# Other homes for squares, normalised rows, token rows and gathered rows, and a nineteenth weight buffer, in a two-layer mixture-of-experts diffusion step

## The reference

```
for l in range(2):
    mod = silu(c) @ w_ada[l] + b_ada[l]                  # 6 x 1024 values, for context and for latent tokens
    h = rms_norm(x) * (1 + scale) + shift
    o = [neighbourhood attention (8 heads), latent attention (8 heads)](h) @ w_out[l]
    x = x + gate1 * o
    h = rms_norm(x) * (1 + scale2) + shift2
    pick 2 of 16 experts for each token                   # router, best group of 4, top 2 in it
    x = x + gate2 * sum over the 2 experts of w * (silu(h @ w_gate[l, e]) * (h @ w_up[l, e])) @ w_down[l, e]
y = rms_norm(x)
```

## Time and profile before

| | |
|---|---|
| time, median of 3 runs | 1088.46 us (1087.3 to 1090.33) |
| the profiled execution: its time, its span | 1087.94 us, 1086.1 us |
| PE busy | 979.1 us (90% of the span) |
| DVE, ACT, POOL busy | 336.8, 247.5, 123.2 us |
| weight queue q1 | 289.06 MB; all queues 314.24 MB, 289 GB/s over the span |

### The profile page before, as it was taken

One profiled execution on the slowest core, in us unless ns is written; L12 is line 12 of the kernel. 1 busy time (PEld: TensorE's weight loads), 2 busy tenths in 40 slices (PEclk: granted clock), 3 DMA queues, 4 the chain that ended last, 5 costly groups with the idle time before them and its releaser, 6 DMA issues. The chain is left out here.

```text
span 1086.1 us, 14414 instructions
## 1 busy us (share of the span) xinstructions
PE 979.1 (90%) x5609; PEld 470.8 (43%) x5609; DVE 336.8 (31%) x858; ACT 247.5 (23%) x591; POOL 123.2 (11%) x140
## 2 busy tenths in 40 slices
PE   4899889998999999888589998999988999988895
PEld 2445546554443433333244554566543333333332
DVE  2200376512732112121240015753146212211225
ACT  2110155412211111111230203553031111111123
POOL 4120200000111111010013002000011111111103
PEclk8999999999999999899889999999989999999999
DMA  9952376663599999999987026667539999999992
GB/s 352 391 194 78 112 281 220 225 272 134 197 369 392 389 390 393 403 402 410 370 331 258 19 94 239 237 228 269 196 117 315 386 385 394 388 410 406 409 402 116
DMA packets 68860, 314.24 MB, mean 289 GB/s; under 512 B 7514, under 2 KB 9782, under 8 KB 47280
## 3 DMA queue, kind: packets, MB, share of 16 engines
q1 hardware_dynamic: 60304, 289.06, 69.4%
q0 software_dynamic: 7616, 21.01, 5.6%
q10 hardware_dynamic: 864, 3.15, 0.7%
HBM read 301.06 MB, written 17.53 MB: 293 GB/s over the span
## 5 line engine op out<-in xcount | busy, mean ns | idle before, releaser
L1032 PE MATMUL psum<-arena 128*64 128x512 f32 x512 | 239.1, 615 | 28.6 <-DMA arena<-in_w_up 24.7
L1035 PE MATMUL psum<-arena 128*64 128x512 f32 x512 | 239.7, 616 | 0.0
L1032 PEld LDWEIGHTS psum<-arena 128*64 128x64 f32 x512 | 69.3, 141 | 178.0 <-issue 173.6
L1088 PE MATMUL psum<-arena 128*64 128x512 f32 x512 | 118.7, 600 | 2.7 <-ACT arena L1538 1.6
L1936 DVE SCALAR_TENSOR_TENSOR arena<-arena,psum 64x512 f32<-64x512 f32 (+1 forms) x32 | 23.9, 748 | 275.5 <-ACT arena L1532 275.5
L1399 PE MATMUL psum<-arena 128*128 128x384 f32 x256 | 86.3, 491 | 0.0
L1253 PE MATMUL psum<-arena 128*128 128x384 f32 x256 | 83.5, 487 | 1.2 <-PE psum L1253 0.6
L1532 ACT ACTIVATE arena<-psum 64x512 f32<-64x512 f32 (+1 forms) x32 | 20.6, 644 | 276.1 <-PE psum L1035 276.1
L1035 PEld LDWEIGHTS psum<-arena 128*64 128x64 f32 x512 | 69.3, 141 | 0.0
L1253 PEld LDWEIGHTS psum<-arena 128*128 128x128 f32 x256 | 48.3, 190 | 36.8 <-issue 4.0
L1399 PEld LDWEIGHTS psum<-arena 128*128 128x128 f32 x256 | 47.5, 190 | 32.4 <-issue 0.7
(11 more groups left out here) (289 smaller groups left out, 1186.4 us busy)
## 6 DMA issues: line engine op xcount, KB each, us to landing
arena<-in_w_gate SPq DMA_DIRECT2D x64, 1024.0 KB, 24.2
arena<-in_w_up SPq DMA_DIRECT2D x54, 1024.0 KB, 23.0
arena<-in_w_ada SPq DMA_DIRECT2D x24, 2048.0 KB
arena<-in_w_down SPq DMA_DIRECT2D x44, 1024.0 KB, 23.0
arena<-in_w_down SPq DMA_DIRECT2D x40, 512.0 KB, 20.6
arena<-in_w_in SPq DMA_DIRECT2D x6, 2048.0 KB
arena<-in_w_up SPq DMA_DIRECT2D x20, 512.0 KB
arena<-in_w_out SPq DMA_DIRECT2D x4, 2048.0 KB
```

The source lines that it names most:

```text
L1032: ins = nc.tensor.matmul(bank[b][0:MAIN, :], hg[:, k, 0:MAIN], row(wg[half], k), start=(k == 0), stop=(k == KD - 1))
L1035: ins = nc.tensor.matmul(bank[b][MAIN:P, :], hg[:, k, 0:MAIN], row(wu[half], k), start=(k == 0), stop=(k == KD - 1))
L1088: ins = nc.tensor.matmul(bank[6][MAIN * j:MAIN * j + MAIN, :], hidT[:, c, 0:MAIN], down_row(w[half], c)[:, 512 * j:512 * j + 512], start=( ...
```

## The change

Memory is dealt out anew so that more places are free when attention ends, and one more place exists. The squares of the second norm of a layer go to `late_squares` (the keys' part of `latent_flat`), and its normalised rows straight into `hT`, where they are modulated in place. So `wide` is free when attention ends: it becomes place 13 and half of 14. Token rows `htok` move to the two result buffers and to `xg[0]`, which now lies in `hT`; so the front of `latent_flat` becomes free at the same time (places 16, 17), with some small rows as 17's other half. Place 18 is new: the rest of `hT`, the tail of `latent_flat` and `ada_rows`. Pieces for down of unit 2 are loaded before those of unit 3. The rows that come back at the end of a layer go to `extra` (places 8 to 11), the final gate and gain rows to `wide`.

```diff
-END_PLACES = (6, 7, 10, 11)
+END_PLACES = (8, 9, 10, 11)
+GATE_PLACES = (13, 14)
...
-NSMALL = 18
-SPLIT = (14, 15, 17)
-ROUND = (0, 1, 2, 3, 8, 9, 10, 11, 12, 15, 4, 5, 6, 7, 13, 14, 16, 17)
+NSMALL = 19
+SPLIT = (14, 15, 17, 18)
+ROUND = (0, 1, 2, 3, 8, 9, 10, 11, 13, 14, 12, 15, 16, 17, 4, 5, 6, 7, 18)
...
     order = gate_up(0) + gate_up(1) + down(0) + gate_up(2) + down(1)
-    for u in range(3, AHEAD):
+    order += down(2) + gate_up(3)
+    for u in range(4, AHEAD):
         order += gate_up(u) + down(u - 1)
...
-        htok = tiles(latent_flat[:, 0:3072], NT)
+        late_squares = tiles(latent_flat[:, 3072:6144], KD)
...
-        xg = [wide[:, 1024 * i:1024 * i + 1024] for i in range(2)]
+        xg = [hT_flat[:, 1024 * i:1024 * i + 1024] for i in range(2)]
+        htok = [y_sb[0], y_sb[1], xg[0]]
...
-        gate_row = [ring[:, 4 * SMALL + D * s:4 * SMALL + D * s + D] for s in range(2)]
-        gain_row = ring[:, 5 * SMALL:5 * SMALL + D]
-        end_hi = tiles(ring[:, 6 * SMALL:6 * SMALL + NT * D], NT)
+        gate_row = [wide[:, D * s:D * s + D] for s in range(2)]
+        gain_row = wide[:, 2 * D:3 * D]
+        end_hi = tiles(extra[:, 0:NT * D], NT)
...
-        y_hi = htok
-        y_lo = tiles(wide, NT)
+        y_hi, y_lo = end_hi, end_lo
...
-                flat = {12: bias_flat, 13: hT_flat, 16: latent_flat}[p][:, 0:SMALL]
+                flat = {12: bias_flat, 13: wide, 16: latent_flat}[p][:, 0:SMALL]
...
-            halves = {14: (bias_flat[:, SMALL:SMALL + 1024], hT_flat[:, SMALL:SMALL + 1024]),
+            halves = {14: (bias_flat[:, SMALL:SMALL + 1024], wide[:, SMALL:SMALL + 1024]),
                       15: (latent_in, caches_flat),
-                      17: (latent_flat[:, SMALL:SMALL + 1024], wide[:, SMALL:SMALL + 1024])}[p]
+                      17: (latent_flat[:, SMALL:SMALL + 1024], small_rows),
+                      18: (hT_flat[:, SMALL:SMALL + 1024], latent_and_rows[:, 8704:9728])}[p]
...
         def squares(n):
-            return xn if n % 2 else hT
+            return late_squares if n % 2 else hT
+
+        def normed(n):
+            return hT if n % 2 else xn
...
                 gate_up_weights(l, 2, 2)
+                down_weights(l, 1, 1)
+                down_weights(l, 2, 2)
                 sp.wait_ge(htok_ps, 2 * NT * (l + 1))
-                down_weights(l, 1, 1)
                 sp.wait_ge(ordered, l + 1)
...
-                sp.wait_ge(h_stored, 16 * NT * (l + 1))
-                sp.wait_ge(first_ps, 2 * (l + 1))
-                before = FIXED - 1
-                for u in range(FIXED, AHEAD):
+                before = ranked(FIXED)
+                gate_up_weights(l, FIXED, before)
+                for u in range(FIXED + 1, AHEAD):
...
-                sp.wait_ge(slot_free, max(loads.last(l, p) for p in (16, 17)) + 1)
+                sp.wait_ge(slot_free, max(loads.last(l, p) for p in END_PLACES) + 1)
                 for t in range(NT):
                     sp.dma_start(y_hi[:, t, :], y_rows.ap()[P * t:P * t + P, :]).then_inc(y_hi_in[t], 16)
-                    if t == 0:
-                        sp.wait_ge(xt_ps, UNITS_E * l + E_ALL)
...
+                act.wait_ge(h_stored, 16 * NT * (l + 1))          # ACT, copy_slots of unit 0
...
+                dve.wait_ge(h_stored, 16 * NT * (l + 1))          # DVE, route, before last_two
```

More of the change, by code:

```diff
@@ L664, in end_again @@
                 sp.wait_ge(stored_y, 32 * NT)
-            sp.wait_ge(slot_free, max(loads.last(DEPTH - 1, p) for p in (4, 5)) + 1)
+            sp.wait_ge(slot_free, max(loads.last(DEPTH - 1, p) for p in GATE_PLACES) + 1)
             sp.dma_start(gain_row, a["final_norm_g"].partition_broadcast(P)).then_inc(gain_in, 16)
@@ L1650, in _ @@
                         t = j // 2
[L1651 removed]
+                        act.dma_start(h_rows.ap()[P * t:P * t + P, :], htok[t]).then_inc(h_stored, 16)
                 experts(l, list(range(AHEAD)), ends=l == DEPTH - 1)
@@ L1968, in gate_diagonals @@
             def gate_diagonals():
-                dve.wait_ge(slot_free, max(loads.last(DEPTH - 1, p) for p in (4, 5)) + 1)
+                dve.wait_ge(slot_free, max(loads.last(DEPTH - 1, p) for p in GATE_PLACES) + 1)
                 each = [P, KD, P]
```

33 lines of the change are left out of this document (17 added, 16 removed).

## The result

The changed kernel takes 1081.76 us (median of 5 runs, 1079.78 to 1083.6), the kernel before, on the same chip, 1090.05 (5 runs, 1087.3 to 1091.91). The ratio is 0.9929, with a 95% interval from 0.9911 to 0.9948: faster by 7.7 us, 5.7 to 9.7. Five runs of the kernel before have their median 1.6 higher, so the gain, 7.7 for 9.3, is the fairer comparison. The profiled execution of the changed kernel took 1082.6 us with a span of 1080.8, against 1087.94 and 1086.1 before. Lines have moved: the gate product is L1038 (before L1032), the down product L1094 (L1088), SP's weight loads L560 (L552), the step behind the branch L510 (L502).

A forecast was written before the change was run, and what follows sets the result against it. Streamed weights were taken to bound the expert stage. Gains of 4.5 + 4.1 - 0.6 + 1.3 = 9.3 us from the profiled 1087.94 gave 1078.6, or 1079.2 as median (0.5 above); range 1075.0 to 1084.5.

The forecast's parts named there:

- The stream bounds the expert stage: Expert stages: streamed weights are the bound; each MB moved into idle time before ends the stage 1/0.396 = 2.5 us sooner.
- Layer 1, 4.1 us, less 0.3 for halves: Layer 1's expert stage: 1.63 MB more moved about point 0 saves 4.1 us; halved pieces cost 0.3.
- Layer 0, 4.5 us, less 0.3: Layer 0's expert stage: 1.76 MB more moved about point 0 saves 4.5 us; halved pieces cost 0.3.
- the points themselves stay where they are in time: Expert stage: points where SP sends further pieces, point 0 the first, do not shift, since PE isn't waiting for weights there.
- Halved pieces, 0.3 us a layer: Weight stream: 20 pieces a layer in halves instead of 15 make smaller packets, costing 0.3 us, from nothing to 0.5.
- The new waits for `h_stored`, nothing: ACT's copy of unit 0's rows: the third token store lands in 2.6 us, before 818, so the wait costs nothing.
- the rival of the slow store: ACT's copy of unit 0's rows: the store still takes 8 us, 1.9 us lost in each layer, 1083; chance 0.03.
- The end of layer 0, w_ada 7.6 us later at no cost: Layer boundary: layer 1's `w_ada` loads wait for the last down product, in at about 556; cost nothing, at most 2 us.
- The code fetch, 1.3 us: PE's gap before `combine`: its code fetch stands behind `w_ada`; sending that later gives 1.3 us, from nothing to 2.7.
- the fetch meets an almost empty queue: PE's branch at the end of layer 0: with `w_ada` sent only at 534, little stands ahead of the code fetch.
- A blocked head of the queue: SP's in-order issue: a unit 6 piece waits for down of unit 2's place, about 6 us lost a layer, 1091.9; chance 0.07.

The follow-up runs named there:

- e1: Changed kernel with 18 homes for weights instead of 19, all 18 pieces still sent as soon as attention ends; 1087.6 us, ratio to before 0.998.
- e5: Changed kernel with the pieces in places 8 to 11 also loaded as halves; 1086.02 us, ratio to before 0.9971.
- e11: Changed kernel's new homes and `h_stored` waits, but 18 homes, old order of first pieces and SP's old waits; 1093.41 us, ratio to before 1.0036.
- e2: Changed kernel with down of unit 1 sent after the tokens' transposes and down of unit 2 after `ordered`; 1087.6 us, ratio to before 0.9977.
- e3: Changed kernel without PE's overflow branch at the end of layer 0; 1081.43 us, ratio to before 0.9917.
- e4: Changed kernel with layer 1's four `w_ada` loads sent only when `combine` has made its first column; 1086.82 us, ratio to before 0.9984.
- e8: Changed kernel with the last down piece in place 3, one `w_ada` load sent early and three after PE's branch; 1079.4 us, ratio to before 0.9901.
- e12: Changed kernel with only the last down piece moved to place 3, so the first `w_ada` load goes out early; 1082.42 us, ratio to before 0.9945.

## Why the prediction was right, and where it was off

**The stream bounds the expert stage.** Right. The DMA share from 311 to 520 and from 842 to 1027 us stayed at 1.02, and one MB more moved before point 0 was worth 2.0 and 3.6 us in layers 0 and 1 (e1 against the changed kernel), 2.65 by the forecast.

**Layer 1, 4.1 us, less 0.3 for halves.** Right: 334.8 and 334.6 became 330.4 and 331.0, 4.0 in the mean. Point 0 was in time in all four. The bytes were 1.79 MB for 1.63, worth 0.4 us more, so the halves may have cost more than 0.3.

**Layer 0, 4.5 us, less 0.3.** The step "the points themselves stay where they are in time" failed for point 0. It came 1.5 us later behind the copy (8.71 for 7.21), because the clock fell there, and the new kernel has nothing left to move while it waits. The bytes were somewhat more than forecast (2.03 MB for 1.76). From the copy on the layer gained 4.2 us where the point was in time, and 1.7 less where the new kernel had it late. The low clock is not peculiar to the new kernel, since the kernel before shows it too; that the stream now depends on point 0 alone is an effect of the change.

**Halved pieces, 0.3 us a layer.** That they cost something is shown by e5. The size is 0.3 to 0.4 if it goes by halved pieces, 0.6 to 0.8 if it goes by halved gate and up pieces; which, the runs don't settle.

**The new waits for `h_stored`, nothing.** Right here, for the reason given: the store lands in 2.6 us because the loads that delayed it are through. e11 and e2 show the other side, the rival of the slow store: with down of unit 1 in front of the store the copy waits for it in both layers. The rival's price, 1.9 us a layer, was too low: taking the late loads away (e11 to e1) was worth 6.1 us, about 3 a layer. It left out that PE's longer idle time, 2.0 us, brings 6.8 us of low clock.

**The end of layer 0, w_ada 7.6 us later at no cost.** It was sent 6.2 us later (7.5 as seen from the end of the last down product) and PE did not wait for it. But the cover is as thin as it was called: in e3, where PE comes 3.3 us sooner, it waits for the loads behind it.

**The code fetch, 1.3 us.** This term was wrong: the gap did not shrink (8.26 to 8.66). The mechanism was right, as e3, e4, e8 and e12 show together, and the size that it can have is 3 us. The step that failed is "the fetch meets an almost empty queue". PE reads the flag at 533.0, `w_ada` goes out at 532.91, and the packet moves behind it at 538. The Trainium skill (Runtime: NRT & Kernel Launch, Instruction fetch mechanics) says that a taken branch out of the prefetched window stops the engine until a DMA has fetched its target; the traces agree, with a packet on q8 between flag and `combine` each time that PE branches, and none in e3. The Trainium skill (DMA: Bandwidth & Descriptors, Queues, rings and completion order) has engines take turns between queues packet by packet, by which neither the fetch nor the store should care much for another queue's backlog. The measurements go against that here, 3 us for the fetch and 8.2 against 2.6 us for the store, and they decide.

**A blocked head of the queue.** It is there, 8.8 us long, and costs nothing, since the backlog at that point was long enough.

**Sum.** 4.2 us a layer with point 0 in time, 1.7 less for each late one in the new kernel, nothing at the boundary: from 5.0 to 8.4 us, and 6.7 if half of the passes are late (an estimate from the table and the 10 of 20), against 7.7 (5.7 to 9.7) measured. The forecast of 9.3 is over by the fetch (1.3) and by what a late point 0 takes. That each layer's 4.2 is the forecast's to a few tenths is partly luck: more bytes and dearer halves may cancel in it.

## What to carry to other kernels

Count what a queue has moved when the next buffer comes free, not what has been issued: here one MB, by one experiment, was 2 to 3.6 us of a stage that is bound by its stream. When everything has been loaded ahead, the event that frees the first buffer becomes the start of the stream, and each us by which it is late now counts. A wait that has been moved to another engine is only as cheap as the transfer behind it, so look at what that transfer queues behind; and keep large loads out of the queues while an engine crosses a branch.

## What the runs showed of the hardware that was not expected

- Large loads sent just before a taken branch hold its code fetch up: TensorE's gap is 8.0 to 8.7 us with `w_ada` in the queues (ten profiles) and 5.7 to 5.9 without (two). The instruction packet moves 4.0 to 5.5 us behind the load of the flag in the ten, 1.5 to 2.5 without.
- TensorE's granted clock falls to its lower level for 3.4 us behind two idle times of 0.7 and 0.8 us in some passes and not in others (10 of 20), at the same place of the same kernel. Behind an idle time of 2.0 to 2.1 us it was low for 6.8 us in three passes of three; behind one of 1.12 us it did not fall. Two products of 0.59 us in these idle times kept it up in all four passes that had them.
- At a full DMA share, the same loads in twice as many halves move at 389 to 390 GB/s, not 391 to 393.
